# Expert weights laid out by contiguous rows: a two-model transformer kernel on one core

## The reference

```
logits = t @ router_w                    # t: 256 x 1024, 16 experts
gates  = top-2 of the best group of four, normalised sigmoid scores
h = einsum('td,edf->tef', t, w_gate_up)  # per expert 1024 x 512
a = silu(h[..., :256]) * h[..., 256:] * gates[..., None]
y = einsum('tef,efd->td', a, w_down)     # per expert 256 x 1024
x = layer_norm(alpha * x + y, ...)
```

## Time and profile before

| what | value |
|---|---|
| median of three runs | 1653.85 us (1653.47 to 1654.48) |
| the profiled execution's own time | 1654.48 us |
| its span | 1652.7 us |
| TensorE busy / VectorE / ScalarE | 94% / 50% / 43% of the span |
| mean rate of the DMA engines | 198 GB/s |
| expert stage of layer 0, first gate/up product to last scatter | 171.3 to 291.8 us |
| expert stage of layer 1 | 457.8 to 578.0 us |

### The profile page before, as it was taken

One profiled execution on the slowest core, in us unless ns is written; L12 is line 12 of the kernel. 1 busy time (PEld: TensorE's weight loads), 2 busy tenths in 40 slices (PEclk: granted clock), 3 DMA queues, 4 the chain that ended last, 5 costly groups with the idle time before them and its releaser, 6 DMA issues.

```text
span 1652.7 us, 22338 instructions
## 1 busy us (share of the span) xinstructions
PE 1561.5 (94%) x7510; PEld 1197.8 (72%) x7510; DVE 827.7 (50%) x1097; ACT 705.8 (43%) x1139; POOL 89.1 (5%) x156
## 2 busy tenths in 40 slices
PE   6988899898889989999999999999999999999997
PEld 5876344687634468887887788877888788778885
DVE  4664222656422264544576555446555556764554
ACT  5662112465111244444555444435444455554443
POOL 2320000041000000000200000000000020000000
PEclk9997999899799989999999999999999999999999
DMA  7525799352589945555625455545555553645551
GB/s 232 191 101 203 277 395 389 99 201 85 203 305 394 385 171 196 178 193 169 204 97 184 165 191 179 192 164 179 188 193 178 188 172 104 202 158 190 187 184 58
DMA packets 194229, 327.43 MB, mean 198 GB/s; under 512 B 8811, under 2 KB 106833, under 8 KB 193633
## 3 DMA queue, kind: packets, MB, share of 16 engines
q1 hardware_dynamic: 193360, 323.52, 56.8%
q0 software_dynamic: 784, 2.85, 0.6%
HBM read 325.28 MB, written 1.05 MB: 197 GB/s over the span
## 4 chain that ended last, share of the span: by engine, by line
issue 65%; PE 24%; DMA 3%; DVE 3%; ACT 2%; DVEq 1%; POOL 1%; SPq 1%; POOLq 1%; ACTq 0%
PE bank L1068 6%; PE bank L1113 3%; PE bank L409 3%; PE bank L410 3%; PE bank L411 3%; DMA sb_moe<-exp_w_down 2%; PE bank L786 1%; PE bank L1027 1%; PE bank L1028 1%; DMA sb_raw<-w_in 1%; PE bank L1123 1%; PE bank L1124 1%; PE bank L890 1%; ACT sb_arena L1408 1%; SPq L500 0%
## 5 line engine op out<-in xcount | busy, mean ns | idle before, releaser
L405 DVE TENSOR_TENSOR sb_wlo<-sb_raw,sb_whi 128x1024 fp32r<-128x1024 f32 (+2 forms) x422 | 486.9, 1197 | 399.3 <-ACT sb_whi L400 398.8
L400 ACT ACTIVATE sb_whi<-sb_raw 128x1024 fp32r<-128x1024 f32 (+2 forms) x424 | 412.9, 1027 | 338.3 <-PE bank L411 330.3
L409 PE MATMUL bank<-sb_whi,sb_op_hi 128*128 128x512 f32 (+2 forms) x1248 | 489.5, 392 | 14.5 <-DVE sb_op_lo L1744 6.5
L411 PE MATMUL bank<-sb_whi,sb_op_lo 128*128 128x512 f32 (+2 forms) x1248 | 482.3, 386 | 0.0
L410 PE MATMUL bank<-sb_wlo,sb_op_hi 128*128 128x512 f32 (+2 forms) x1248 | 482.0, 386 | 0.0
L409 PEld LDWEIGHTS bank<-sb_whi,sb_op_hi 128*128 128x128 f32 x1248 | 236.1, 189 | 63.4 <-DVE sb_op_lo L2031 8.1
L411 PEld LDWEIGHTS bank<-sb_whi,sb_op_lo 128*128 128x128 f32 x1248 | 235.8, 189 | 48.1
L410 PEld LDWEIGHTS bank<-sb_wlo,sb_op_hi 128*128 128x128 f32 x1248 | 236.3, 189 | 45.1
L409 PE MATMUL bank<-sb_whi,sb_lat_hi 128*128 128x512 f32 (+2 forms) x424 | 162.8, 384 | 7.1 <-DVE sb_lat_lo L1720 6.0
L411 PE MATMUL bank<-sb_whi,sb_lat_lo 128*128 128x512 f32 (+2 forms) x424 | 162.1, 382 | 0.0
L410 PE MATMUL bank<-sb_wlo,sb_lat_hi 128*128 128x512 f32 (+2 forms) x424 | 161.9, 382 | 0.0
(11 more groups left out here) (234 smaller groups left out, 1257.0 us busy)
## 6 DMA issues: line engine op xcount, KB each, us to landing
sb_raw<-ffn_w SPq DMA_DIRECT2D x264, 512.0 KB, 4.4
sb_moe<-exp_w_gate_up SPq DMA_DIRECT2D x64, 1024.0 KB, 9.6
sb_raw<-w_in SPq DMA_DIRECT2D x84, 512.0 KB, 4.6
sb_moe<-exp_w_down SPq DMA_DIRECT2D x32, 1024.0 KB, 10.2
sb_raw<-w_out SPq DMA_DIRECT2D x32, 512.0 KB, 4.5
sb_raw<-w_branch_pool SPq DMA_DIRECT2D x8, 512.0 KB, 4.1
sb_raw<-w_branch_attn SPq DMA_DIRECT2D x8, 512.0 KB, 7.3
sb_raw<-w_in SPq DMA_DIRECT2D x8, 288.0 KB, 7.2
```

The costliest lines, as they stand in the source:

```text
L400: nc.scalar.activation(h, r, ACT.Copy).then_inc(hi_made.sem, 1)
L405: nc.vector.tensor_tensor(o, r, h.bitcast(F32), ALU.subtract).then_inc(lo_made.sem, 1)
L409: nc.tensor.matmul(ps, hi, wh, start=first, stop=False)
L411: return nc.tensor.matmul(ps, lo, wh, start=False, stop=last)
```

## The change

Row d of the width is now given to block d mod 8 and partition d div 8, so that a partition's eight rows are neighbours in memory. `by_k` becomes "(q k)": block k is every eighth column of `x`, a step of 32 bytes. The slab of `exp_w_gate_up` is cut as "(p k) n", and `exp_w_down` as "(p f) n": a partition's part of every expert slab is one piece of 8 KB. (Of a gate/up slab this piece is half of the 16 KB that the partition has of that expert; of a down slab the pieces join to 1 MB.) `router_w` is loaded by the same map, in pieces of 512 bytes in place of 64. `activated` writes value 2 q + f to column 128 f + q of block f, reading its inputs in order and writing in two streams that lie 512 bytes apart.

`y_hi` and `y_lo` become tiles of their own, and `op_hi` and `op_lo` move into the memory that the expert stage reuses. Signals, waits, counts of instructions and sizes stay as they were.

```
-        op_hi = sb("op_hi", [P, DK, T], F32R)
-        op_lo = sb("op_lo", [P, DK, T], F32R)
...
+            op_hi = turn.enter_context(nc.sbuf_tensor("sb_op_hi", [P, DK, T], F32R))
+            op_lo = turn.enter_context(nc.sbuf_tensor("sb_op_lo", [P, DK, T], F32R))
...
-        y_hi, y_lo = (t[:, :, :].rearrange("p (b k) t -> p b (k t)", b=2) for t in (op_hi, op_lo))
+        y_hi, y_lo = sb("y_hi", [P, 2, D], F32R), sb("y_lo", [P, 2, D], F32R)
...
-        by_k = lambda t: t.rearrange("p (k q) -> p k q", k=DK)
+        by_k = lambda t: t.rearrange("p (q k) -> p k q", k=DK)
+        by_f = lambda t: t.rearrange("p (q f) -> p q f", f=2)
+        as_rows = lambda t: t.rearrange("p (f q) -> p q f", f=2)
...
-  w = a["exp_w_gate_up"][...].rearrange("l e (k p) n -> p (l e k) n", p=P)[:, 4 * h:4 * h + 4, :]
+  w = a["exp_w_gate_up"][...].rearrange("l e (p k) n -> p (l e k) n", k=DK)[:, 4 * h:4 * h + 4, :]
...
-  w = a["exp_w_down"][...].rearrange("l e (f p) n -> p (l e f) n", p=P)
+  w = a["exp_w_down"][...].rearrange("l e (p f) n -> p (l e f) n", f=2)
...
-  (rw[:, 0:DK * NE].rearrange("p (k n) -> p k n", k=DK), a["router_w"].rearrange("(k p) n -> p k n", p=P)),
+  (rw[:, 0:DK * NE], a["router_w"].rearrange("(p k) n -> p (k n)", k=DK)),
...
-  return stt(out=out, in0=b[:, FE:2 * FE], scalar=gate, in1=silu, op0=ALU.mult, op1=ALU.mult)
+  return stt(out=as_rows(out), in0=by_f(b[:, FE:2 * FE]), scalar=gate, in1=by_f(silu), op0=ALU.mult, op1=ALU.mult)
```

More of the change, by code:

```diff
@@ L492, in expert_slab @@
                         e, h = 2 * p + n % 2, n // 2
-                        w = a["exp_w_gate_up"][bass.ds(l, 1), e:e + 1, :, :].rearrange("l e (k p) n -> p (l e k) n", p=P)[:, 4 * h:4 * h + 4, :]
+                        w = a["exp_w_gate_up"][bass.ds(l, 1), e:e + 1, :, :].rearrange("l e (p k) n -> p (l e k) n", k=DK)[:, 4 * h:4 * h + 4, :]
                         dst = dst.rearrange("p (k n) -> p k n", n=2 * FE)
@@ L496, in expert_slab @@
                         e = 2 * (p - 1) + n % 2
-                        w = a["exp_w_down"][bass.ds(l, 1), e:e + 1, :, :].rearrange("l e (f p) n -> p (l e f) n", p=P)
+                        w = a["exp_w_down"][bass.ds(l, 1), e:e + 1, :, :].rearrange("l e (p f) n -> p (l e f) n", f=2)
                         dst = dst.rearrange("p (f n) -> p f n", n=D)
```

## The result

The changed kernel takes 1672.1 us (1669.4 to 1674.3, 4 runs) where the kernel before takes 1653.7 in the same session: a ratio of 1.0106, 95% interval 1.0093 to 1.0119. It is slower by 18 us; 1652.8 was forecast, and "slower" had a chance of 0.20. The profiled execution took 1669.62 us, its span is 1667.8. Lines of the changed kernel are 2 higher than before's from `by_k` on (L409 to L411 are now L411 to L413, L1068 is L1070, L1113 is L1115).

What follows compares the result with a forecast made beforehand. TensorE was taken as the bound, busy 94% of the span, with DMA also full in the expert pairs. Loads -1.97, transposes +0.7 and activated +0.2 gave -1.1 us, from 1653.85 to 1652.8 us, range 1649.5 to 1658.

Steps and rivals of the forecast that it cites:

- The moved tiles: New addresses of op_hi, op_lo, y_hi and y_lo, with waits, counts and sizes unchanged: zero cost.
- The loads: Expert slab loads in 8 KB pieces: 5 to 10% faster, ending TensorE's stalls, gain 1.97 us, bounds 0 and 1.97.
- the three stalls: TensorE's losses to expert loads: 0.83 us and 0.30 us in layer 0's pairs, 0.84 us in layer 1; all to go.
- The transposes: TensorE's eight transposes a chunk read x at 32-byte steps: first chunk covered, second 0.35 us a layer, +0.7 us in all.
- `xs_hi` and `xs_lo`: ScalarE and VectorE passes reading at 32-byte steps: 0.70 ns more an element, covered by 0.5 us, so zero.
- `activated`: Activation written in two alternating streams: 0 to 0.18 us a layer in pair 0, 0.1 taken, +0.2 us in all.
- The clock: Rival: the gather's half-clock stretch is absent, 1649.3 us (chance 0.12), or comes once more, 1656.3 us (chance 0.09).
- The steps are dear: Rival: a 32-byte step costs four times a neighbouring element in transposes and xs_lo, 1663 us; chance 0.12.
- slow loads: Rival: 8 KB out of every 16 KB meets memory less evenly; 10% slower expert loads give 1674 us; chance 0.05.

Runs made afterwards that it cites:

- e1: The kernel before with only op_hi and op_lo moved and y_hi and y_lo made tiles of their own: 1673.8 us, ratio 1.0115.
- e2: The changed kernel with op_hi and op_lo back in their old place, sharing memory with y_hi and y_lo again: 1651.7 us, ratio 0.9986.
- e10: The kernel before with only the two slab maps of the expert loads changed, for timing alone: 1651.7 us, ratio 0.9980.
- e5: The changed kernel with 128 unused bytes below op_hi, so op_hi and op_lo start like the weight slabs modulo 256: 1653.2 us, ratio 0.9993.
- e11: The changed kernel with the op and y tiles in their old place and the old expert slab maps, for timing alone: 1654.7 us, ratio 1.0003.
- e6: The kernel before with 128 unused bytes below op_hi, putting op and lat tiles on multiples of 256, slabs at 128: 1678.7 us, ratio 1.0149.
- e7: The changed kernel with 128 bytes below everything, putting slabs and lat tiles on multiples of 256, op tiles at 128: 1670.6 us, ratio 1.0098.
- e9: The changed kernel with 192 bytes below op_hi, so op tiles start 64 bytes above the slabs modulo 256: 1671.7 us, ratio 1.0103.
- e12: The changed kernel with 96 bytes below op_hi, so op tiles start 32 bytes below the slabs modulo 256: 1672.8 us, ratio 1.0113.
- e14: The changed kernel with 160 bytes below op_hi, so op tiles start 32 bytes above the slabs modulo 256: 1674.2 us, ratio 1.0119.

## Why the prediction was wrong

**The step that failed** is "The moved tiles": "Nothing in the trace depends on an address that I can see; zero." It is about +19 us: e1 alone gives 1.0115, and after over e2 is 1.0106 / 0.9986 = 1.012. By the rows it is 3744 products x 4.8 ns = 18 us. I had the count and the period of these products before me and put no price on their operands' place, as the trace of one kernel can't show what another place would cost. What I could have had: a term of unknown size on the largest group of instructions. Each nanosecond on those 3744 products is 3.7 us, more than all the terms of the sum together, so that a zero there needed a bound and had none.

**The loads**: right. -1.97 us was forecast, the three stalls are gone, and e10 measures -1.8 to -4.6. About 1 us of its median is more than the stalls, but its interval begins at 1.8, so no run shows that it is more. The rate of a busy DMA engine in the pairs is 409 / (16 x 0.99) = 25.8 GB/s against 23.7, 9% more; 5 to 10% was taken. The Trainium skill (DMA: Bandwidth & Descriptors, Why small descriptors are slow) had given 3 to 4%, an estimate that holds for the pieces of 2 KB; with the third in 4 KB it is under 3%. The trace shows more than twice as much as either. Neither changes the sum, since TensorE is the bound as soon as the stalls are gone.

**The transposes**: +0.7 us was forecast. The first chunk takes 1.16 us against 1.09, with cover; the second, at the half clock, 1.97 as before. So nothing: 0.07 us where it is hidden.

**`xs_hi` and `xs_lo`**: dearer than taken. ScalarE's pass goes from 1.05 to 2.07 us, 1.0 ns an element, VectorE's from 1.23 to 2.08, 0.83 ns. Whether that is covered depends on TensorE's clock in the gather. In the changed kernel's trace the gather ran at the full clock, its first round was over by 162.5, and `in_slot` came at 163.5: a wait of 1.13 us before 163.61, where I had counted 0.5 us of cover. In e2's and e5's traces most of the first round ran at the half clock and no such wait stands. The Trainium skill (SBUF — State Buffer, the note on cachelines) says that each access that crosses to a new 16-byte line pays a penalty. The rows agree: with a step of 32 bytes each element crosses, and on ScalarE and VectorE it costs about twice (2.07 us against 1.05), not four times as in the rival.

**`activated`**: 675 ns against 484, 0.75 ns for each written element, and TensorE's wait in pair 0 is 1.47 us against 1.30. That is 0.17 us a layer, the upper bound; 0.1 was taken.

**The clock**: the rival is there in part. The first 32 products of the gather ran at the full clock, but the wait for `in_slot` took nearly all of it back: from the first start to the last it is 168.94 - 160.42 = 8.52 us, where it was 8.76. The stretch at the half clock came in pair 0 instead, whose 32 products take 8.78 us where the other groups take 7.09, as pair 0 did before: 1.69 us lost.

**The other rivals.** "The steps are dear" named 1663 and "slow loads" 1674; the second number is near the result, but for a reason that is not there. (The sum of the dear steps is also off: three times the 1.23 us of `xs_lo` is 3.7 us and not 3.2, half a microsecond more a layer.) Steps and loads together are e2, a gain of 2.3 us at the medians, where -1.1 was forecast. Had the tiles stayed in step, as in e5 (1653.2), the forecast of 1652.8 would have stood. That would have been right in total and not proof of the terms: e10 gives -2.9 for the loads against -1.97, e11 gives +0.1 for the steps against +0.9, and both intervals, some 1.4 us each way, hold the forecast. e5 is also the version to keep if the separate `y` tiles are wanted; e2 has the lowest median with all of the new maps in it, 1651.7, but its interval overlaps e5's.

## What to carry to other kernels

When a change moves an operand of the main products, read where the compiler puts it before and after, and keep the stationary tile and the streamed tile equal modulo 256 bytes; a pad of 128 bytes was worth 19 us here. That is shown for products of 128 x 128 by 512 columns on tiles declared `float32r`; for other shapes and types measure it with such a pad. A part of a change that is "only bookkeeping" but touches the largest group of instructions gets a bound from that group's count, not a zero. And run such a part by itself first: e1 and e2 settled in two runs what the profile of the whole change leaves mixed.

## What the runs showed of the hardware

- At a granted clock of 1.00, products of 128 x 128 by 512 columns, on tiles declared `float32r`, follow each other 227 ns apart when both operands start alike modulo 256 bytes, and 232 to 234 ns apart when they don't (e6, e7, e9, e12, e14 and after); 64 bytes below, about 229.
- The products of the pairs, whose stationary tile has 64 columns, don't show it. `xg` starts on a multiple of 256 in the changed kernel and 128 after one in e6, with the slabs at 128 in both, so it is off in the first and alike in the second. A group of 32 takes 7.09 us in both; the changed kernel's row at 272.42 stands above, and this is e6's:

```profile
270.37 7.09 PE L1069 MATMUL bank<-sb_moe,sb_xg 128*64 128x512 f32 x32
```

- The page's busy time of the weight loads doesn't show it either: 1197.8 us before, 1197.7 after, for 17 us more of products.
- A step of 32 bytes in the stationary operand costs a transpose next to nothing (0.07 us for eight at the full clock, none seen at the half), while it costs ScalarE and VectorE 1.0 and 0.83 ns an element.
